# Two-layer hybrid decoder trunk: the key/value modulation group summed on GpSimd, the output product begun inside the head pairs, sines and loads moved

## The reference

```python
for l in range(2):
    mod = silu(c) @ ada_w[l] + ada_b[l]              # (1, 6*1024)
    sh1, sc1, g1, sh2, sc2, g2 = split(mod, 6)
    if l == 1:                                       # shared keys and values
        kvmod = silu(c) @ kv_ada_w + kv_ada_b        # (1, 2*1024): shift, scale
        h = rms_norm(x, kv_norm_g) * (1 + scale) + shift
        down = h @ kv_w_down                         # latent 256, rotary key 32
        k, v = up-projections, key norm, rotary embedding with cos/sin of pos
    h = rms_norm(x, norm1_g[l]) * (1 + sc1) + sh1
    y = dilated_attention(h) @ a_w_o  if l == 0 else  mla_attention(h, k, v) @ b_w_o
    x = x + g1 * y
    h = rms_norm(x, norm2_g[l]) * (1 + sc2) + sh2
    x = x + g2 * moe_ffn(h)        # sigmoid router, 64 experts, top 6, one shared expert
```

## Time and profile before

| | |
|---|---|
| median of three runs | 1338.48 us |
| profiled execution, its own time | 1336.37 us |
| its span, first to last instruction | 1334.6 us |
| PE busy | 1102.6 us, 83% |
| DVE busy | 439.1 us, 33% |
| ACT busy | 252.9 us, 19% |
| POOL busy | 0.4 us |
| read from HBM | 500 MB, mean 375 GB/s |
| chain that ended last | SP's queue 45%, PE 33%, DMA 9%, DVE 6% |

### The profile page before, as it was taken

How to read it: one execution, slowest core, us unless ns; L and a number is a source line. 1 busy time by engine, 2 the same in 40 slices (tenths; PEclk the granted TensorE clock), 3 DMA queues, 4 the chain that set the end, 5 groups by cost and what they waited for, 6 DMA issues and landing times.

```text
span 1334.6 us, 17222 instructions
## 1 busy us (share of the span) xinstructions
PE 1102.6 (83%) x6664; PEld 613.9 (46%) x6664; DVE 439.1 (33%) x1028; ACT 252.9 (19%) x572; POOL 0.4 (0%) x5
## 2 busy tenths in 40 slices
PE   5999899998787778877679889999868888867776
PEld 4886477454233323333237468745323333423332
DVE  1297765221112112111137866622111212111213
ACT  1122613111101111011022372311011101110100
POOL 0000000000000000000000000000000000000000
PEclk9998999999889899889889999999889989988988
DMA  9996979999999999999986756589999999999994
GB/s 349 385 405 276 368 287 362 380 425 423 423 424 425 423 423 424 424 425 422 423 329 247 284 190 245 228 351 426 422 424 424 425 423 423 424 424 424 424 424 203
DMA packets 99915, 502.26 MB, mean 376 GB/s; under 512 B 11866, under 2 KB 37367, under 8 KB 44535
## 3 DMA queue, kind: packets, MB, share of 16 engines
q1 hardware_dynamic: 99366, 500.92, 92.1%
q10 hardware_dynamic: 464, 0.20, 0.1%
HBM read 500.04 MB, written 1.05 MB: 375 GB/s over the span
## 4 chain that ended last, share of the span: by engine, by line
SPq 45%; PE 33%; DMA 9%; DVE 6%; issue 4%; ACT 2%; DVEq 0%; ACTq 0%
SPq L598 42%; PE bank L733 26%; DMA w_gu<-in_moe_w_gate_up 6%; SPq L687 3%; PE bank L1121 2%; PE bank L736 2%; DMA w_gu_x<-in_moe_w_gate_up 2%; DMA ring<-in_ada_w 2%; PE bank L956 1%; ACT p_sb L1357 1%; PE bank L1102 1%; PE bank L879 1%; DVE s_sb L1635 0%; DVE x L1854 0%; DVE y_lo L1803 0%
## 5 line engine op out<-in xcount | busy, mean ns | idle before, releaser
L733 PE MATMUL bank<-w_gu,ring 128*32 128x512 f32 (+1 forms) x1088 | 343.7, 698 | 80.3 <-DMA w_gu<-in_moe_w_gate_up 54.5
L733 PEld LDWEIGHTS bank<-w_gu,ring 128*32 128x32 f32 (+1 forms) x1088 | 90.3, 134 | 213.6 <-issue 213.6
L733 PE MATMUL bank<-ring 128*32 128x512 f32 (+1 forms) x384 | 161.5, 690 | 21.0 <-DMA w_gu<-in_moe_w_gate_up 20.8
L1786 DVE TENSOR_TENSOR hh<-sg,bank 128x256 f32<-128x256 f32 x44 | 27.4, 624 | 429.5 <-ACT sg L1388 429.5
L733 PE MATMUL bank<-w_gu_x,ring 128*32 128x512 f32 (+1 forms) x320 | 144.0, 666 | 25.9 <-DMA w_gu<-in_moe_w_gate_up 21.7
L733 PE MATMUL bank<-w_gu,hhT 128*32 128x512 f32 (+1 forms) x576 | 147.2, 599 | 1.4 <-DMA w_gu<-in_moe_w_down 1.2
L733 PE MATMUL bank<-w_dn,ring 128*32 128x512 f32 x240 | 103.8, 808 | 26.3 <-DMA w_gu<-in_moe_w_gate_up 10.7
L1803 DVE SCALAR_TENSOR_TENSOR y_lo<-bank,w_slot,y_hi 128x512 fp32r<-128x512 f32 x88 | 62.0, 746 | 174.3 <-ACT y_hi L1280 174.3
L1388 ACT ACTIVATE sg<-bank 128x256 f32<-128x256 f32 x44 | 16.9, 385 | 507.4 <-PE bank L733 507.4
L733 PE MATMUL bank<-sel,h_hi 128*128 128x256 f32 x352 | 87.7, 289 | 0.0
L733 PE MATMUL bank<-sel,h_lo 128*128 128x256 f32 x352 | 84.2, 279 | 0.0
(11 more groups left out here) (291 smaller groups left out, 1571.5 us busy)
## 6 DMA issues: line engine op xcount, KB each, us to landing
w_gu<-in_moe_w_gate_up SPq DMA_DIRECT2D x126, 1024.0 KB, 25.9
w_gu<-in_moe_w_down SPq DMA_DIRECT2D x68, 1024.0 KB, 26.3
ring<-in_moe_w_gate_up SPq DMA_DIRECT2D x44, 1024.0 KB, 26.7
w_gu_x<-in_moe_w_gate_up SPq DMA_DIRECT2D x38, 1024.0 KB, 25.2
ring<-in_ada_w SPq DMA_DIRECT2D x36, 1024.0 KB, 10.2
w_dn<-in_moe_w_gate_up SPq DMA_DIRECT2D x30, 1024.0 KB, 25.7
ring<-in_moe_w_down SPq DMA_DIRECT2D x16, 1024.0 KB, 26.1
w_dn<-in_moe_w_down SPq DMA_DIRECT2D x14, 1024.0 KB, 26.7
```

What stands on the lines that cost most here:

```text
L733: return nc.tensor.matmul(o, a, b, start=first, stop=last)
L1786: v.tensor_tensor(hh[:, :].rearrange("s (f p) -> s p f", f=FE // P), sg[:, :].rearrange("s (p f) -> s p f", f=FE // P), bank[b][:, FE:2 * ...
```

## The change

1. Group 6 leaves the ring and PE. Its eight chunks are loaded into units 8, 9, 0, 1, 2, 3, 10, 11 (`ada_6`), in which the first experts' weights are put later. POOL multiplies each by silu(c) and adds it to the first: eight `tensor_scalar` and seven `tensor_tensor` instructions of 128 x 2048, each behind a wait on the one before it. PE's sum over partitions is put behind output chunk 1, the turn into columns behind chunk 2.
2. The first output chunk is accumulated in three pieces (`first_output`), two of them inside the last steps of the head pairs, in both layers; its PSUM bank is 0, that of chunk 1 is bank 1.
3. The sines (ACT, L1447) are put from the end of the query/key/value stage to its chunk 8.
4. SP's order changes with the buffers; since group 6 no longer takes part in the ring, later chunks fall on other slots.
5. A semaphore of its own between two DVE instructions (`slots`) becomes DVE's common chain semaphore.

```diff
-        for g in (1, 2, 6):
+        for g in (1, 2):
             ada_chunks(g, 0, KT)
...
-        SUMS_TURN = {1: 1, 2: 2, 3: 3, 4: 4, 5: 5}
+        SUMS_TURN = {1: 1, 2: 2, 6: 3, 3: 4, 4: 5, 5: 6}
...
+        ADA_6_UNIT = (8, 9, 0, 1, 2, 3, 10, 11)
+        ada_6 = [unit_at[0][u] for u in ADA_6_UNIT]
...
-        WO_BANK = (2, 3, 4, 5)
+        WO_BANK = (0, 1, 4, 5)
...
+            def ada_6_loads(k0, k1):
+                for k in range(k0, k1):
+                    sp.dma_start(ada_6[k].rearrange("p (a n) -> p a n", a=1),
+                                 t["kv_ada_w"].rearrange("(p k) n -> p k n", k=KT)[:, k:k + 1, :])\
+                      .then_inc(sem(f"unit_in{ADA_6_UNIT[k]}"), 16)
...
-                    load_chunks(order[9:number[("wo", 0, 1)] + 1])
-                    fixed_loads(0, EARLY_UNITS[0:2])
+                    load_chunks(order[9:16])
+                    ada_6_loads(0, 2)
                     sp.wait_ge(sem("qkv_ps"), 8)
-                    fixed_loads(0, EARLY_UNITS[2:4])
-                    load_chunks(order[number[("ada", 3, 3)]:number[("ada", 3, 6)] + 1])
+                    ada_6_loads(2, 4)
+                    load_chunks(order[16:number[("wo", 0, 1)] + 1])
                     sp.wait_ge(sem("qkv_ps"), 10)
-                    fixed_loads(0, EARLY_UNITS[4:6])
-                    load_chunks([("ada", 3, 7)])
+                    ada_6_loads(4, 6)
+                    sp.wait_ge(sem("qkv_ps"), 12)
+                    ada_6_loads(6, 8)
+                    sp.wait_ge(sem("ada_6_used"), 5)
+                    fixed_loads(0, EARLY_UNITS[1:5])
+                    load_chunks(order[number[("ada", 3, 3)]:number[("ada", 3, 5)] + 1])
+                    load_chunks([("ada", 3, 6), ("ada", 3, 7)])
+                    sp.wait_ge(sem("ada_6_used"), KT)
+                    fixed_loads(0, EARLY_UNITS[5:8])
                     sp.dma_start(w_router[:, :, :, :].rearrange("p l k e -> p (l k) e"),
                                  t["moe_w_router"].rearrange("l (k p) e -> p (l k) e", p=P)).then_inc(sem("router_in"), 16)
                     for n in range(2):
...
-                    sp.wait_ge(sem("qkv_ps"), 12)
-                    fixed_loads(0, EARLY_UNITS[6:8])
+                    sp.wait_ge(sem("ada_sums"), SUMS_TURN[6])
+                    fixed_loads(0, EARLY_UNITS[0:1])
                     load_chunks([("sgu", 0, 1)])
...
+                def first_output(k0, k1):
+
+                    w = use(("wo", l, 0))
+                    for k in range(k0, k1):
+                        pe.wait_ge(sem("o_sb"), pairs + k + 1)
+                        for ti in range(NT):
+                            last = nc.tensor.matmul(bank[WO_BANK[0]][:, ti * N:(ti + 1) * N], hT[:, k, ti * P:(ti + 1) * P], w[:, k, :],
+                                                    start=k == 0 and ti == 0, stop=k == KT - 1, skip_group_check=True)
+                    if k1 == KT:
+                        used(("wo", l, 0), last)
...
-                        if l == 0 and 2 <= g < 6:
-                            ada_steps(6, 2 * g - 4, 2 * g - 2)
-                        if l == 0 and g == 6:
-                            ada_columns(6)
...
-                pe.wait_ge(sem("o_sb"), pairs + H // 2)
-                for c in range(4):
+                    if g == H // 2:
+                        first_output(0, 4)
+                    if g == H // 2 + 1:
+                        first_output(4, 6)
+
+                first_output(6, KT)
+                for c in range(1, 4):
...
+                    if l == 0 and c == 1:
+                        ada_sums(6)
+                    if l == 0 and c == 2:
+                        ada_columns(6)
...
             for c in range(12):
                 if c == 8:
                     ada_rows(1)
+                    act.wait_ge(sem("angles"), 1)
+                    for a in range(2):
+                        last = nc.scalar.activation(sincos[:, a, :, :], ang[:, 2 + a, :, :], ACT.Sin)
+                    last.then_inc(sem("sines"), 1)
...
-                    if g == 7 and l == 0:
-                        modulation(6, 4, 104, col("kv_norm_g", 0, 8))
...
                     v.tensor_tensor(xs, xs, gj, ALU.add).then_inc(sem("x_part"), 1)
+                    if l == 0 and c == 2:
+                        modulation(6, 4, 104, col("kv_norm_g", 0, 8))
...
+            pool.wait_ge(sem("csilu"), 1)
+            for k in range(KT):
+                pool.wait_ge(sem(f"unit_in{ADA_6_UNIT[k]}"), 16)
+                scaled = nc.gpsimd.tensor_scalar(ada_6[k], ada_6[k], csilu[:, k:k + 1], None, ALU.mult)
+                if k == 0:
+                    scaled.then_inc(sem("ada_6_used"), 1)
+                else:
+                    scaled.then_inc(sem("rows_zero"), 1)
+                    pool.wait_ge(sem("rows_zero"), k + 1)
+                    nc.gpsimd.tensor_tensor(ada_6[0], ada_6[0], ada_6[k], ALU.add).then_inc(sem("ada_6_used"), 1)
+                pool.wait_ge(sem("ada_6_used"), k + 1)
```

More of the change, by code:

```diff
@@ L448, in wo_chunk, with sgu_chunk @@
                 chunk(("wo", l, j), wo[:, :, j * 256:(j + 1) * 256], KT, 256)
-            def sgu_chunks():
-                for j in range(2):
-                    chunk(("sgu", l, j), sgu[:, :, j * 256:(j + 1) * 256], KT, 256)
+            def sgu_chunk(j):
+                chunk(("sgu", l, j), sgu[:, :, j * 256:(j + 1) * 256], KT, 256)
             g = ADA_IN_WO[l]
@@ L692, in _ @@
                 if l == 0:
-                    for name in (("kvd", 1, 0), ("dq", 1, 0), ("uk", 1, 0)):
+                    for name in sorted((("kvd", 1, 0), ("dq", 1, 0), ("uk", 1, 0)), key=lambda name: (
+                            PASS_OF[USERS[unit_of_ring[ring_of(number[name])]][-1][1]])):
                         wait_read(sp, l, USERS[unit_of_ring[ring_of(number[name])]][-1])
@@ L764, in ada_sums @@
                 pe.wait_ge(sem("gate_sb"), GATES_BY[g])
-                if g == 4:
-                    pe.wait_ge(sem("ada_4_used"), KT)
+                if g in (4, 6):
+                    pe.wait_ge(sem(f"ada_{g}_used"), KT)
                 else:
                     freed(pe, ("ada", g, KT - 1))
-                sums = ada_4[0] if g == 4 else acc
+                sums = {4: ada_4[0], 6: ada_6[0]}.get(g, acc)
                 for q in range(4):
@@ L772, in ada_sums @@
                 last.then_inc(sem("ada_sums"), 1)
-            def ada_steps(g, k0, k1):
-                if k0 == 0:
-                    pe.wait_ge(sem("mod_sb"), ADA_TURN[g])
-                    pe.wait_ge(sem("gate_sb"), GATES_BY[g])
-                for k in range(k0, k1):
-                    w = use(("ada", g, k))
-                    for q in range(4):
-                        last = mm(bank[7][32 * q:32 * q + 1, :], csilu[:, k:k + 1], w[:, 0, q * 512:(q + 1) * 512], k == 0,
-                                  k == KT - 1)
-                    used(("ada", g, k), last)
             def gate_half(n, half, b=7):
@@ L1323, in ada_rows @@
                     act.wait_ge(sem("ada_sums"), SUMS_TURN[g])
-                if g == 6:
-                    after(("ada", g, KT - 1))
                 copy(row_of[g][:, :], bank[7][:, :]).then_inc(sem("row_sb"), 1)
@@ L1344, in attention @@
                 for g in range(H // 2 + 3):
-                    if l == 0 and g == 6:
-                        ada_rows(6)
                     if l == 1 and g == 2:
@@ L1444, in _ @@
                         copy(kT[:, 2 * b - 8:2 * b - 6, :].rearrange("p k n -> p (k n)"), src).then_inc(sem("qkT_sb"), 1)
-            act.wait_ge(sem("angles"), 1)
-            for a in range(2):
-                last = nc.scalar.activation(sincos[:, a, :, :], ang[:, 2 + a, :, :], ACT.Sin)
-            last.then_inc(sem("sines"), 1)
             ada_rows(2)
```

26 lines of the change are left out of this document (15 added, 11 removed).

## The result

The changed kernel takes 1405.37 us (median of four runs, 1399.82 to 1407.18) beside 1339.49 us for the kernel before: ratio 1.0479, 95% interval 1.0458 to 1.0501. It is 66 us slower where 6 us faster was forecast. The time lies above the whole range (1329 to 1364); it is also 45 us above the figure of rival 1. The profiled execution took 1407.18 us, with a span of 1405.4 us.

A forecast was written before the change was run, and what follows sets the result against it. Transfers bound the expert plateaus; ahead of them the chain on PE and DVE through head pairs and output product was priced. Layer 0's 5.66 us and layer 1's 0.57 made 6.2, so 1338.5 - 6.2 = 1332.3 us, range 1329 to 1364.

The forecast's parts named there:

- rival 1: Head pairs, layer 0: DVE and POOL exclude each other for whole instructions; 21.6 us slower, 1360.1 us (1337 to 1383), chance 0.32.
- The forecast's own sum: Both layers: gains in layer 0 of 5.66 us plus layer 1's, 6.2 us in all, giving 1332.3 us.
- 5.7 for the sines and group 6: Layer 0 up to the last pair: 1.25 us from moving the sines, 4.47 from taking group 6 off PE.
- the case that the text put at half of 4.47: Head pairs: if PE's clock drops while less busy, PE sets the pace again and half the gain is lost.
- 0.57 - 2.09 + 1.46: Output product, layer 0: first chunk gains 0.57 us, group 6's sum and columns cost 2.09, earlier loads gain 1.46.
- Layer 1's small term: Layer 1's output product: PE's idle 0.57 us ahead of the last values is filled.
- The zero end is what the forecast takes: Head pairs: POOL working beside DVE was priced at no disturbance, 0 us.
- POOL's 50 us: POOL's eight scalings and seven additions for group 6, from about 108 us: middle of 26.7 and 72.6 us.
- the upper bound, 72.6 us: POOL's work on group 6 priced from its 0.20 us row scaled by 16: 3.3 us one stream, 6.6 two.
- Group 3's chunk 3 waits for DVE's use of chunk 0, right after the pairs, before and after: Loads, layer 0: same wait as before, chunk lands by about 180 us; output product's final 1.46 us wait goes.
- Rival 3: Loads, layer 0: units or group 3's last chunk come late, gain given back; 1336 us, chance 0.10.
- Rivals 2 and 3: The first: POOL too slow at 72.6 us, PE waits for its sum, 1338.5 us, chance 0.06; the second: Rival 3.

The follow-up runs named there:

- both: Changed kernel with POOL's fifteen instructions cut to 2 columns and DVE's first step of group 3 waiting for group 2's sum: 1332.25 us.
- the last experiment: Kernel before, plus only the first output chunk begun inside the pairs and the sines at chunk 8: 1337.68 us.
- the last two experiments: Changed kernel with group 6 on PE from the units, POOL empty: 1333.92 us; kernel before plus only early first output chunk and moved sines: 1337.68 us.
- additions alone: Changed kernel, group 3 waiting for group 2's sum, POOL's seven additions whole and eight scalings on 2 columns: 1353.57 us, once.
- writes-only kernel: Changed kernel, group 3 waiting for group 2's sum, POOL's fifteen instructions replaced by memsets of 128x2048: 1345.62 us, once.

## Why the prediction was wrong

**The forecast's own sum came out, but not term by term.** Everything but POOL's work and one wait gives 1332.25 us. Step by step, in the profile of "both": the last pair's position term stands at 152.33 us for 157.36, 5.0 us of the 5.7 for the sines and group 6. The steps from the third term on take 20.7 us for the forecast's 18.95: once they are 6.0 us apart, where DVE waits 2.35 us for PE at a clock of 0.67, the case that the text put at half of 4.47. On the other side the third term comes 2.3 us earlier, not 1.25. From the last term to x the forecast had 0.57 - 2.09 + 1.46, in sum nothing, and the trace has 0.25 us: output product through at 191.51 (forecast 191), x at 193.04 (193), first reload at 223.34 (224.5), group 3's last chunks issued from 169.20 on. The end moved by 4.9 us in the profiled span and by 8 in the medians. Layer 1's small term can't be read apart from that scatter.

That the sum fits to 0.1 us is partly luck. In the last experiment group 6 is still on PE, and its last position term stands at 153.25 us: 4.1 of the 5.0 us are there already. The third term stands at 131.56 for 133.94, so 2.4 us came with moving the sines, and not 1.25. From the third to the last term it took 21.7 us, for 23.42 before. The 1.7 us between them are mostly the last step, in which PE of the kernel before needed 1.55 us for twelve rows of values and here 0.88; from 150 to 160 us its granted clock was 0.83 before and 0.95 here. Taking group 6 off PE then brought 21.7 - 20.7 = 1.0 us of the pairs' time in these profiles, where the sum had 4.47; 2.2 us of the difference are the step of 6.0 us at the low clock. Nor do single profiles agree on the rest. From x complete to the first reload, where nothing was changed, it took 31.9 us before, 30.3 with both edits, and 33.2 and 33.3 in the last two experiments. How the 8 us divide among the parts stays open.

**First failed step: "The zero end is what the forecast takes".** The likeliest case was given to no disturbance, because no row showed one. The exclusion is real, and the largest number of this case: 54.7 us. Its condition stood in rival 1 word for word, POOL beside DVE while DVE sets the pace of the pairs. The rule stood in the prediction, DVE was seen to be full, and "no row shows it" is no evidence against a rule whose situation the old kernel never had. That was a chance wrongly weighed, 0.32 where it should have been most.

**Second: rival 1's price.** It put DVE through at 185.1 us; it was 211.54. The term that was mis-sized is POOL's 50 us: fifteen instructions took 78.8, the additions 4.50 to 4.54 and the scalings 5.55 to 7.29 us each. The additions agree with the Trainium skill's 4.5 us ("GPSIMD Engine Reference", "Elementwise — side-by-side cycle accounting"). A scaling had been put at 2.3 us as cheaper than an addition, as it is on DVE, and is dearer. Even the upper bound, 72.6 us, was too low. POOL also began at 113.98 us and not 108. With both corrected, the rival's row of POOL and DVE work gives 185.1 + 28.8 + 6.0 = 219.9 us, 8 more than measured; 4.7 of the 8 are two of its four steps of group 2, which were done before POOL began. Taken by pairs: while POOL worked, four steps from 125.88 to 194.69 us took 68.8 us for 15.2 at 3.79, which is 53.6 us of the 54.7.

DVE's rows say which instructions pay (changed kernel, 110 to 210 us):

```profile
L1652 DVE CUSTOM_DVE_ANT_0 s_sb<-s_sb,cst 128x256 f32<-128x256 f32 x16 | 24.7, 1543 | 0.0
L1652 DVE CUSTOM_DVE_ANT_0 s_sb<-s_sb,cst 128x128 f32<-128x128 f32 x16 | 13.3, 829 | 0.3
...
L1646 DVE SCALAR_TENSOR_TENSOR s_sb<-negrel,bank 128x384 f32<-128x384 f32 x16 | 8.1, 546 | 3.2 <-PE bank L751 3.2
...
L1656 DVE TENSOR_SCALAR nmax<-smax 128x4 f32<-128x4 f32 x8 | 6.1, 765 | 0.9
```

The mask steps took 38.0 us for 11.3 before, and the scalings of the exponentials 36.5 for 10.1; `nmax`, overlapping its neighbours, 6.1 for 1.4. The position term reads one input from SBUF and one from PSUM, and is unchanged at 546 ns.

The rival let the two exclude each other for their whole length. That holds for the additions; a scaling lets DVE through once. It also holds the other way round. DVE's last two steps on `acc` for group 2, 2.35 us each by themselves, met POOL's first scalings. In the changed kernel (min/median/max in ns) and with POOL's work cut to 2 columns, POOL's row and then DVE's:

```profile
L2059 POOL TENSOR_SCALAR w_gu_x<-w_gu_x,csilu x2: 5629/6458/7287, 114.0 to 121.4; 128x2048 f32<-128x2048 f32 x2
```

```profile
116.48 2.43 POOL L2059 TENSOR_SCALAR w_gu_x<-w_gu_x,csilu 128x2 f32<-128x2 f32 x1 [2.17 <-DMA w_gu_x<-in_kv_ada_w]
```

```profile
114.11 4.73 DVE L1576 SCALAR_TENSOR_TENSOR acc<-ring,csilu,acc 128x2048 f32<-128x2048 f32 x2
```

A scaling of two columns, 0.29 us elsewhere, took 2.43 us and ended with DVE's step (118.91 and 118.84 us).

**Third: "Group 3's chunk 3 waits for DVE's use of chunk 0, right after the pairs, before and after".** It is right after the pairs only if DVE may start. Its first step waits for the sum one turn before its own, so that `acc` is free. Before, the turn ahead of group 3's was group 2's, long past. Now group 6 has a turn in between, though it doesn't use `acc` at all, and its sum stands on PE behind output chunk 1. The edit to one table of numbers moved a wait whose own line the diff does not show. It costs 17.6 us with POOL's work taken out and 18.4 with it, and neither the forecast nor a rival had it: it was put at nothing. Rival 3 came nearest (a late chunk of group 3) with 1336 us as its price.

**Rivals 2 and 3.** PE never waits for POOL: the last addition ends at 193.97 and the sum is made at 230.63, so POOL was not late for it, but only because the engines that it held up came later still. Rival 3's mark, PE waiting for a transfer, is there at 243.61, as a result of the third step.

**Open.** From the last load of layer 0 (64.3 us late) to the end (70.8 in the span) another 6.5 us are lost, in layer 1. PE's granted clock is 0.76, 0.89 and 0.83 in the three stretches of 10 us from 844 to 874 us of the changed kernel, and 1.00 in the kernel before from 780 to 810 us, the same place 64 us earlier. Whether the change causes those dips was not tried apart.

## What to carry to other kernels

An idle engine is not a free engine: before POOL gets work beside DVE, list DVE's instructions in that stretch by their operands, and price each POOL instruction that reads as a stop for those with two SBUF inputs or at double rate (here 54.7 us for 78.8 us of POOL's work). Where DVE sets the pace, what it is held up lands on the time. Before work is given to another engine, try a new place on the same one: group 6 kept on PE but fed from other buffers brings, with the two small parts, the 6 us that the forecast had for the whole change. And where a table of turns is edited, follow every `turn - 1` that reads it.

## What the runs showed of the hardware

- A POOL `tensor_scalar` with a per-partition factor, 128x2048 float32, took 5.44 us at the least and 5.55 to 5.84 in most rows of the changed kernel; a `tensor_tensor` 4.50 to 4.59; a memset 1.80 to 1.90.
- A DVE row of the kinds that are held up grows by what is left of the POOL instruction beside it, whatever its own size: a `nmax` of 128x4 took 4.26 us beside an addition. Additions and scalings alternating without a pause cost more (54.7 us) than the two kinds measured alone (21.3 and 24.8 us, single runs). Why was not tried; in the trace of additions alone POOL has pauses.
- Memsets on POOL held up DVE's one-input scaling (683 for 284 ns) and not its two-input step (290 ns).
- POOL can be the one that waits: its first scaling of the changed kernel took 7.29 us and one of two columns 2.43 us, both begun while a two-input step of DVE was running. Beside the shorter rows of the pairs POOL's rows hardly grew (additions 4.50 to 4.59 us), so there the price is seen on DVE's rows.
- PE's granted clock was 0.50 from 160 to 180 us of the changed kernel, where PE was busy for 2.60 of 20 us. In the writes-only kernel it was 0.50 from 140 to 160 us, and the first 16 rows of the output product then took 5.22 us, for 3.72 in the kernel of both edits. That the late DVE brought this second dip about is not shown: with both edits the clock was 0.67 from 130 to 140 us.
